# A decoder layer with routed experts: loads of the attention stage moved in time, routing and experts joined into one block, and a score lead that grows from 72 to 104

## What is computed

```
def block(args):                      # differential attention, 8 heads, head dim 2 x 64, v dim 128
    s = einsum(q, k) * scale + bias;  s = where(rel >= 0, s, -inf)
    p = softmax(s);  a = p[0] - lam * p[1]
    return einsum(a, v)
o = rms_norm(o, subln_g) * (1 - lambda_init);  x = x + o @ w_out
g_idx = argmax(softmax(ht @ w_group + b_group));  top 2 of the 8 experts of the group
y += w * ((silu(xb @ w_gate[e]) * (xb @ w_up[e])) @ w_down[e])   # for both experts of a token
```

## Time and profile before

| | us |
|---|---|
| three runs | 2559.82, 2561.47, 2563.64 |
| the profiled execution | 2560.01 |
| its span, first to last instruction | 2558.4 |
| PE busy | 2315.9 (91%) |
| DVE busy | 1371.7 (54%) |
| ACT busy | 1217.1 (48%) |
| POOL busy | 753.4 (29%) |

### The profile page before, as it was taken

The page is one execution under the profiler, slowest core; times in us unless marked ns, Lnnn a source line. Parts: engine busy times, 40 slices in busy tenths (PEclk is TensorE's granted clock), DMA queues, the critical chain, the costliest instruction groups (busy, mean ns, idle before and its releaser), DMA issues. The chain is left out here.

```text
span 2558.4 us, 36873 instructions
## 1 busy us (share of the span) xinstructions
PE 2315.9 (91%) x11480; PEld 1853.9 (72%) x11480; DVE 1371.7 (54%) x2803; ACT 1217.1 (48%) x1640; POOL 753.4 (29%) x686
## 2 busy tenths in 40 slices
PE   4999999997999999999959998389999999999981
PEld 3888889996666676666647887367888888788760
DVE  6212121103777777677535666567664655666763
ACT  5111111113677777777634444365564555565653
POOL 0000000003777777778600111222222222122220
PEclk7999999998999999999979998699999999999995
DMA  5333334226334443442045332679887878888857
GB/s 190 132 115 129 108 127 132 63 65 155 77 79 114 114 106 98 102 118 73 20 167 190 115 131 83 230 252 349 288 307 239 276 221 305 287 302 297 306 164 279
DMA packets 207629, 441.46 MB, mean 173 GB/s; under 512 B 19081, under 2 KB 56113, under 8 KB 205490
## 3 DMA queue, kind: packets, MB, share of 16 engines
q1 hardware_dynamic: 188530, 379.46, 44.0%
q0 software_dynamic: 19008, 60.91, 9.4%
HBM read 338.55 MB, written 101.76 MB: 172 GB/s over the span
## 5 line engine op out<-in xcount | busy, mean ns | idle before, releaser
L1400 DVE TENSOR_TENSOR gu_lo<-gu_raw,gu_hi 128x2048 fp32r<-128x2048 f32 x128 | 293.3, 2291 | 129.6 <-issue 79.1
L548 POOL TENSOR_TENSOR p_ring<-p_ring 128x512 f32<-128x512 f32 (+2 forms) x192 | 334.3, 1741 | 16.0
L608 DVE TENSOR_SCALAR_CACHE_REDUCE p_ring<-ps_s 128x512 f32<-128x512 f32 (+6 forms) x352 | 277.2, 792 | 114.5 <-PE ps_s L679 108.6
L573 ACT ACTIVATE p_ring<-p_ring,shift 128x1152 f32<-128x1152 f32 (+15 forms) x256 | 306.0, 1198 | 30.8 <-DVE shift L624 30.8
L716 PE MATMUL ps_o<-aT,v_st 128*128 128x512 f32 (+3 forms) x640 | 287.2, 531 | 0.0
L1342 ACT ACTIVATE gu_hi<-gu_raw 128x2048 fp32r (+1 forms) x128 | 237.8, 1914 | 28.6 <-PEq L767 15.4
L562 ACT ACTIVATE aT<-ps_t 128x512 f32<-128x512 f32 (+1 forms) x320 | 168.7, 531 | 171.1 <-PE ps_t L701 169.9
L1474 PE MATMUL ps_g<-gu_hi,xT_lo 128*128 128x512 f32 x720 | 235.5, 408 | 7.5 <-DVE xT_lo L1415 7.5
L1474 PE MATMUL ps_g<-gu_lo,xT_hi 128*128 128x512 f32 x720 | 227.4, 397 | 0.0
L1474 PE MATMUL ps_g<-gu_hi,xT_hi 128*128 128x512 f32 x720 | 226.8, 396 | 0.0
L545 POOL TENSOR_SCALAR p_ring<-p_ring,coef 128x512 f32<-128x512 f32 (+2 forms) x192 | 167.9, 875 | 150.5 <-DVE coef L637 146.3
(11 more groups left out here) (218 smaller groups left out, 4374.6 us busy)
## 6 DMA issues: line engine op xcount, KB each, us to landing
gu_raw<-in_moe_w_gate SPq DMA_DIRECT2D x128, 512.0 KB, 8.9
gu_raw<-in_moe_w_up SPq DMA_DIRECT2D x128, 512.0 KB, 10.0
d_raw<-in_moe_w_down SPq DMA_DIRECT2D x64, 1024.0 KB, 7.1
qk<-stage SPq DMA_DIRECT2D x64, 512.0 KB, 2.8
q_first<-qk SPq DMA_DIRECT2D x64, 256.0 KB, 5.1
q_second<-qk SPq DMA_DIRECT2D x64, 256.0 KB, 5.1
w_raw<-in_diff_w_in POOLq DMA_DIRECT2D x12, 1024.0 KB, 6.7
k<-qk SPq DMA_DIRECT2D x8, 1024.0 KB, 12.4
```

What stands on the lines that cost most here:

```text
L548: pool.tensor_tensor(p0(r, c0, c1), p0(r, c0, c1), p1(r, c0, c1), ALU.add).then_inc(mixed, 1)
L573: nc.scalar.activation(p, p, ACT.Exp, bias=shift[:, r % 8, m:m + 1], accum_out=sums[:, r % 8, m:m + 1]).then_inc(raised, 1)
L608: ins = nc.vector.tensor_scalar(p(r, k0, k0 + far), ps_s[:, c % 2, 0:far], SCALE, None, ALU.mult, ALU.max, accum_out=top[:, r % 4, m, col: ...
L1400: nc.vector.tensor_tensor(gu_lo[:, j * GC:(j + 1) * GC], raw(half, j), gu_hi[:, j * GC:(j + 1) * GC].bitcast(F32), ALU.subtract).then_inc( ...
```

## The change

1. Loads of the second head: k and near of head 1 are issued at slot 0 and v at slot 8; they stood ahead of the stores of `nil`.
2. The lead: 72 up to slot 0, then one more per slot up to 104 at slot 32. `p0_ring` grows from 70 x 256 to 86 x 256 columns, `inv` from 16 to 32 rows. `p1_ring` stays.
3. Loads in attention time: the constants and `sub_g` at slot 40, the first half of Wo when head 6 is scored, and, when all rows are mixed, the first two tiles of the attention output and the second half of Wo (these into `p1_ring`).
4. The start of routing: `sub_gs` waits for two small memsets only; the Wo split is cut in two halves around the first turn, and the first projection waits for each chunk of Wo as it comes; index work moves behind it.
5. One block: routing and experts share one block. The down weights of expert 0 and the gate and up weights of expert 1 are issued after the last projection. POOL lets the scatters of one tile be under way while it issues the next, then waits for all and gathers the first rows without a meeting of the engines. ACT and DVE split expert 0 ahead of the first rows, the down weights behind them.

```diff
-    LEAD = 72
-    P0, P1 = 70 * 256, 24 * 256
+    LEAD0, LEAD = 72, 104
+    P0, P1 = 86 * 256, 24 * 256
...
-        while c < NC and scored_cost < turned_cost + LEAD:
+        while c < NC and scored_cost < turned_cost + min(LEAD, LEAD0 + max(0, n)):
...
             load_q(sp, 1)
             load_v(sp, 0)
-            load_k(sp, 1)
-            load_near(sp, 1)
-            load_v(sp, 1)
...
             for n in range(BEGIN, END):
+                if n == 0:
+                    load_k(sp, 1)
+                    load_near(sp, 1)
+                if n == 8:
+                    load_v(sp, 1)
...
+                if n == CONSTANTS_AT:
+                    sp.dma_start(keep["sub_g"][:, :], io["diff_subln"].rearrange("o p -> p o")).then_inc(gain_in, 16)
...
+                if slot_of[last_piece[16 * (HEADS - 2) + 15]] + 1 == n:
...
+                    sp.dma_start(keep["wo_raw"][0][:, :, :], wo_rows[:, 0:KC // 2]).then_inc(wo_in[0], 16)
                 if n == NU:
 
                     gate(sp, mixed, mixed_parts[NR], passed)
-                    sp.dma_start(keep["wo_raw"], io["diff_w_out"].rearrange("o (c p) n -> p (o c) n", p=P)
-                                 [:, 0:KC // 2]).then_inc(wo_in, 16)
+                    g = quads.index((HEADS - 1, 0))
+                    gate(sp, o_out[g % 2], 16 * (g // 2 + 1), passed)
+                    for t in range(2):
+                        sp.dma_start(keep["o_t"][:, t, :], scratch["o"][t * P:(t + 1) * P, :]).then_inc(o_in[t], 16)
+                    sp.dma_start(keep["wo_raw"][1], wo_rows[:, KC // 2:]).then_inc(wo_in[1], 16)
...
-                                                tokw[:, q, k, :], None).then_inc(scattered, 16)
-                    gate(pool, scattered, t * 32 + 32, passed)
+                                                tokw[:, q, k, :], None).then_inc(scattered[q], 16)
+
+                    gate(pool, scattered[1 - q], t * 16 + SCATTERED0, passed)
...
+            gate(sp, projected, TILES + PROJECTED0, passed)
+            for j in range(DS):
+                sp.dma_start(keep["d_raw"][:, j, :, :], expert_rows(io["moe_w_down"], 0, j, DC)).then_inc(d_in[j], 16)
+            for j in range(GS):
+                load_gate_up(sp, io, keep["gu_raw"][:, 1], gu_in, 1, j)
...
+                if at == 0:
+                    split_low(range(KC // 2))
...
+                            if at == 1 and k < 2 * KC:
+                                pe.wait_ge((wo_hi_set, wo_split)[k // KC], c + 1)
...
-            load_down(0)
-            load_next(1)
+            gate(sp, x_in, 16, passed)
...
             gu_high(0, 0, None, range(GS))
+            x_high(0)
+            act.wait_ge(sem("c_tab_set"), 17)
             d_high(0, None)
             n = blocks_of(act)
-            x_high(0)
...
             gu_low(0, 0, range(GS))
+            x_low(0)
             d_low(0)
             n = blocks_of(dve)
-            x_low(0)
...
-        mix_and_route(nc, io, keep, scratch, sem)
+        routing = mix_and_route(nc, io, keep, scratch, sem)
...
-        run_experts(nc, io, keep, scratch, sem)
+        run_experts(nc, io, keep, scratch, sem, routing)
```

More of the change, by code:

```diff
@@ L978, in step, with route_vector @@
                     nc.scalar.activation(h2T[:, :], ps_c[:, :], ACT.Copy).then_inc(h2T_set, 1)
-            def split_high():
-                for half in range(2):
-                    act.wait_ge(wo_in[half], 16)
-                    for c in range(KC // 2):
-                        nc.scalar.activation(wo_hi[:, half * (KC // 2) + c, :], wo_raw[half][:, c, :],
-                                             ACT.Copy).then_inc(wo_hi_set, 1)
-            steps(act, step, after_first=split_high)
-        @block.vector
-        def _(dve):
+            steps(act, step, after_first=lambda: split_high(range(KC // 2, KC)))
+        def route_vector(dve):
             dve.sem_inc(summed, SUMMED0)
@@ L1150, in _, with turn_h2, route @@
             pe.sem_inc(h2T_set, H2T0)
-            pe.wait_ge(made, 11)
+            def turn_h2(n, par, at):
+                if has(at, 2):
+                    t = n - 2
+                    pe.wait_ge(h2_set, t + 1)
+                    pe.wait_ge(h2T_set, t + H2T0)
+                    for c in range(KC):
+                        mm = pe.transpose(ps_c[:, c * P:(c + 1) * P], h2[:, par, c * P:(c + 1) * P], ident[:, :])
+                    mm.then_inc(turned2, 1)
+            def route(n, at):
+                if has(at, 3):
+                    t = n - 3
+                    pe.wait_ge(h2T_set, t + (1 + H2T0))
+                    if at == 3:
+                        pe.wait_ge(const_in, 16 * 5)
+                    if at > 3:
+                        pe.wait_ge(chosen, t * 13 + -12)
+                    for c in range(KC):
+                        mm = pe.matmul(ps_d[:, 0:ROUTES], h2T[:, c * P:(c + 1) * P], w_r[:, c, :], start=c == 0,
+                                       stop=c == KC - 1)
+                    mm.then_inc(routed, 1)
             def step(n, par, at):
@@ L1171, in step @@
                     mm.then_inc(turned, 1)
[L1172 to L1188 removed]
+                if at < TILES:
+                    turn_h2(n, par, at)
+                    route(n, at)
+                else:
+                    route(n, at)
+                    turn_h2(n, par, at)
                 if has(at, 4):
                     t, q = n - 4, par
+                    if at == 4:
+                        pe.wait_ge(made, 11)
                     pe.wait_ge(both_set, t + (1 + BOTH0))
@@ L1601, in build @@
             keep["xt"] = xt
+        keep["o_t"] = keep["p1_ring"][:, 0:2 * D].rearrange("p (a d) -> p a d", a=2)
+        wo_rest = keep["p1_ring"][:, 2 * D:(2 + KC // 2) * D].rearrange("p (c n) -> p c n", c=KC // 2)
+        with nc.sbuf_tensor("wo_first", [P, KC // 2, D], F32, side="right") as wo_first:
+            keep["wo_raw"] = (wo_first, wo_rest)
         k0 = ctx.enter_context(ExitStack())
```

185 lines of the change are left out of this document (92 added, 93 removed).

## The result

The changed kernel takes **2534.65 us** in the median of 4 runs (2532.33 to 2539.46), the kernel before 2562.55 in four (2559.82 to 2563.89): a ratio of 0.9892, 95% interval 0.9879 to 0.9905, so 28 us or 1.1% less. The prediction said 2535. The profiled execution took 2535.79 us, its span is 2534.2 (before 2560.01 and 2558.4). Where those 24.2 us of span came from, by the same points on PE's, DVE's and POOL's timelines in both profiles (us). A turn-back is the group of four transposes that turns the output of a quad; a turn is the group of eight that turns one tile of routing; the last slot is DVE's last computation of a place in the slot lists.

What follows compares the result with a forecast made beforehand. PE was taken to bound attention (busy 624.8 of 641.3 us), with larger holes at the seams. -7.2 + 1 - 9.1 - 10.3 = -25.6 us on 2560.0 gave 2534.4; with medians 1.5 us higher, 2535 was said, range 2524 to 2549.

Steps and rivals of the forecast that it cites:

- Part 1: Start of attention: with head 1's loads later, PE's wait for the third quad's queries goes, -7.2 us (bounds -7.2 and -4.0).
- Part 2: Attention: the growing lead changes only PE's 16.5 us of gaps and gains nothing, +1 us (bounds -11.6 and +15).
- the bound of -11.6: Attention, best case for the lead: all of PE's 11.6 us of waits for DVE to empty PSUM gone.
- The small fears: Attention: third-quad queries about 1 us late once, POOL just keeping up, constants costing nothing or 1 us once.
- Part 3: Attention to routing: first projection 12.1 us earlier, less 3 us for a later last store, -9.1 us (bounds -12.1 and -7).
- What would show it: The prediction's list of signs on the timelines by which it would be judged right or wrong.
- Part 4: Routing to experts: list issued 3.6 us earlier, list and row landings 3.6 and 3.1 us shorter, -10.3 us (bounds -13 and -3.6).
- A (queries late): Attention: quad 3's load needs longer than the 8 us left, 2.2 us in each of 7 heads, +15, 2550; 12%.
- D (POOL sets the pace): Attention: POOL over 3 us behind stops DVE, then PE; a full mixing in each of 7 heads, +36, 2571; 4%.
- B (the gaps close): Attention: with short rows placed elsewhere the 11.6 us of waits vanish, 2523; 10%.
- C: Routing to experts: list and gathered rows take as long without traffic, +6.7, 2542; 10%.
- E: Lead and single block do nothing, since the chip has something else due at each seam; -10, 2551; 4%.

Runs made afterwards that it cites:

- head1_early: The changed kernel with the loads of head 1 (k, near, v) back ahead of the nil store; 2537.97 us, ratio 0.9907.
- before_head1: The kernel before with only the loads of head 1 issued later; 2558.98 us, ratio 0.9982.
- before_coef: The kernel before with only each coefficient worked out by a tensor_scalar with two scalar operands; 2552.57 us, ratio 0.9963.
- lead72: The changed kernel with the lead held at 72 throughout, ring sizes kept; 2542.59 us, ratio 0.9913.
- before_lead: The kernel before with only the growing lead and the ring, inverses and moved output tile it needs; 2560.95 us, ratio 0.9988.
- loads_late: The changed kernel with the 6 MB for experts 0 and 1 issued after the block table, as in the kernel before; 2540.58 us, ratio 0.9911.
- loads_at_list: The changed kernel with the 6 MB for experts 0 and 1 issued when POOL issues the first list; one run, 2543.0 us.

## Why the prediction was right, and where it was not

The forecast was the likeliest case, -25.6 us, and the profiles differ by 24.2. Its last addition slips: 2534.4 + 1.5 is 2535.9, so the working gave 2536 and not the 2535 that was said. By its own steps:

- **Part 1, -7.2: mechanism right, size 1.4 us too large.** The queries were there at 631.2, as worked out (630.6). The step "so it goes straight on, and all 7.2 us go" skipped PE: DVE's first piece comes 2.2 us after PE's first score (637.09 to 639.30; 631.21 to 633.41 now), so only 5.9 us could come back. head1_early and before_head1 put it at 6.1 and 6.0.
- **Part 2, +1: wrong by 5.7 us, the largest miss.** Two sentences failed. "I see no reason why short rows should stall less: the 14 waits come from two PSUM buffers and DVE's fixed cost per piece": the rows of the 1.1 us waits stand behind a coefficient held by POOL, as the earlier trace rows hinted with its 247 and 1624 ns, and before_coef takes those waits away without touching the lead. The deeper lead takes them away as well, though coefficients are then held for up to 3.2 us; why the pieces wait less there, no run shows. And "at full clock throughout": the 1.00 of the earlier trace rows is a mean over 641 us in which eight at 0.79 do not show. What the runs showed in place of +1: 2.2 us less idle time, 1.7 us of half clock that did not come again, 0.8 us less busy time otherwise. The sum of the waits for `top` did stay (11.6 to 10.7), as I said; it was the wrong thing to count. The sign that attention's gaps stay near 16 us and PE's busy time unchanged did not come true (14.2, and 2.4 us less). lead72 prices the lead at 6.3 us, before_lead at 4.9; the bound of -11.6 held it. The small fears were unfounded: no wait for `q_first` or `q_second` appears in attention, POOL sets no pace (DVE waits for it 4.9 us in all, before 3.1), the constants cost nothing.
- **Part 3, -9.1: right** (-8.9). The load and the store of the earlier trace rows did not both end at 1290.1: the store landed 3.0 us after its issue, at 1290.75, behind the load as the changed kernel's does. Store to block 6.2 us instead of 3.55, +2.6 where I had put 3; ACT started 1.2 us after the block instead of 0.4; the chain from the norm to the first projection took what was added up. The projection itself ran 1.2 us longer, part of it at half clock, which I had not counted. Under "What would show it" I gave 15 us from the last transposes to the first projection; by my own terms it is 27.65 - 9.1 = 18.5, and 18.75 was measured. That sentence had left the 3 us of the store out.
- **Part 4, -10.3: right.** -4.5, -3.6 and -2.7 were measured for -3.6, -3.6 and -3.1; loads_late gives back the third and loads_at_list the second, the first has no run of its own. PE's new order in the last steps gave 0.3 us for the predicted nothing.
- **What had no term: the routing loop, +4.9.** The profile of before had drawn a good one. The lesson is in the working: the sum was made against a single execution whose loop was at the low end of what runs give, so the medians moved by 27.9 us and the profiles by 24.2.
- **The rivals.** A (queries late) and D (POOL sets the pace) did not happen in any profile. B (the gaps close) was right in its sign for 4.7 of its 11.6 us, of which only some 2.2 are gaps that closed. C is out by loads_at_list. E is out.

So 2535 for 2534.65 is partly luck: the lead gave 5.7 us more than forecast and the last seam 0.8, against which stand 1.4 us missing in part 1, 1.4 in part 3 with its first projection, and 4.9 in the loop.

## What to carry to other kernels

Count the waits of the bounding engine by their length and place, not by their sum, and read the clock in stretches of some microseconds around them: a pair of waits of 0.5 to 1.1 us cost 1.7 us more behind it in 3 of 21 places here. When a tiny instruction has a wide spread (218 to 3165 ns), look at what the other engines end at the same instant; changing its form was worth more than the whole reordering of attention. At a seam, ask what the last small store stands behind and whether anybody needs it yet, and, before pricing a part against one profile, look at how far the same stretch varies in others.

## What the runs showed of the hardware that I had not expected

- A scalar_tensor_tensor of one column on DVE with two inputs in SBUF is held until the end of POOL's tensor_tensor over 896 to 1536 columns (1.27 and 3.16 us for 0.22); a tensor_scalar with two scalar operands is not (272 to 277 ns, 121 of 121).
- TensorE fell to half clock behind waits of 1.1 and 0.5 to 0.8 us in a stage otherwise busy for 97%, in some heads and not in others (once in the profile of before, twice in that of lead72, never in that of before_head1, of seven each; 1.7 us lost each time). The waits' lengths do not decide it: 1.09 and 0.74 us at 798 in the profile of before left the clock at 1.00.
- The routing loop varies by 9 us (237.6 to 246.3) between profiles. Its mean granted clock (0.90 to 0.93) makes part of that, idle time on PE (16.8 to 22.3 us) the rest. Much of the 7 to 10 us between the fastest and the slowest run of one kernel may lie there, which was not tested by itself.
- A 256 KB store issued 4.9 us after a 2 MB load on the same queue held the next block 3.2 us longer (6.2 and 2.95 us) than with that load behind it.
